# Postponing the first norm's sums and the first column's evacuation in a two-block kernel on one core

## The reference

```
def rmsnorm(u, g):
    r = rsqrt(mean(u * u, axis=-1) + 1e-6)
    return u * r * g

h = rmsnorm(x, g[0])
z = h @ w_in                      # 2048 x 6144
hy = dwconv3(z[..., :3072], hy_short_w, hy_short_b)
x0, x1, v = split(hy, 3)
h_fwd, h_bwd = hyena_filters(...) # two small sin layers, then a wide one
y_a = x0 * two_sided_fftconv(v * x1, h_fwd, h_bwd, hy_bias)
gb, gc, xv = split(z[..., 3072:], 3)
y_b = gb * dwconv3(gc * xv, sc_conv_w)
m = concatenate([y_a, y_b]) @ w_out
```

## Time and profile before

| what | value |
|---|---|
| median of 3 runs | 2413.16 us (2412.05 to 2413.39) |
| time of the profiled execution | 2412.67 us |
| its span in the profile | 2410.8 us |
| PE busy | 2370.4 us (98%) |
| DVE busy | 1327.5 us (55%) |
| ACT busy | 1096.3 us (45%) |
| POOL busy | 27.7 us (1%) |
| mean granted PE clock | 0.995 of full speed |

### The profile page before, as it was taken

The page is one execution under the profiler, slowest core; times in us unless marked ns, Lnnn a source line. Parts: engine busy times, 40 slices in busy tenths (PEclk is TensorE's granted clock), DMA queues, the critical chain, the costliest instruction groups (busy, mean ns, idle before and its releaser), DMA issues.

```text
span 2410.8 us, 25538 instructions
## 1 busy us (share of the span) xinstructions
PE 2370.4 (98%) x11089; PEld 1961.8 (81%) x11089; DVE 1327.5 (55%) x1315; ACT 1096.3 (45%) x1159; POOL 27.7 (1%) x49
## 2 busy tenths in 40 slices
PE   7999999999999999999999999999999999999998
PEld 6778787788888888888888888888888878888887
DVE  5675855544544544556764454444454576555654
ACT  5444444544454344355555444344334356444443
POOL 1000000000000000000000000000000000000000
PEclk9999999999999999999999999999999999999999
DMA  7444455555555555555445555555555545643344
GB/s 283 170 156 182 176 203 196 181 187 192 192 202 188 187 190 192 192 188 209 184 176 187 192 192 186 191 183 191 192 192 185 190 149 190 248 148 140 122 149 148
DMA packets 63103, 446.08 MB, mean 185 GB/s; under 512 B 7209, under 2 KB 7540, under 8 KB 11215
## 3 DMA queue, kind: packets, MB, share of 16 engines
q1 hardware_dynamic: 60080, 427.60, 49.6%
q0 software_dynamic: 2912, 16.85, 1.9%
HBM read 442.33 MB, written 2.10 MB: 184 GB/s over the span
## 4 chain that ended last, share of the span: by engine, by line
PE 93%; DVE 3%; DMA 2%; ACT 2%; issue 1%; POOL 0%; ACTq 0%; POOLq 0%; SPq 0%; DVEq 0%
PE P L329 90%; PE P L332 3%; DVE raw_r L596 1%; ACT hi L487 1%; DMA raw<-in_w_i 1%; DVE R_h L583 0%; DMA raw<-in_w_z 0%; DMA raw<-in_w_d 0%; DVE X L583 0%; DVE EV L639 0%; ACT R_h L483 0%; DVE R_m L580 0%; DMA raw<-in_w_ukv 0%; ACT EV L509 0%; DMA raw<-in_w_u 0%
## 5 line engine op out<-in xcount | busy, mean ns | idle before, releaser
L596 DVE TENSOR_TENSOR raw_r<-raw,hi 128x2048 fp32r<-128x2048 f32 (+3 forms) x412 | 928.4, 2256 | 954.4 <-ACT hi L487 953.8
L329 PE MATMUL P<-hi,R_h 128*128 128x512 f32 (+2 forms) x3840 | 1231.9, 395 | 17.9 <-DVE raw_r L596 10.9
L487 ACT ACTIVATE hi<-raw 128x2048 fp32r<-128x2048 f32 (+3 forms) x412 | 776.4, 1887 | 1010.9 <-DMA raw<-in_w_d 390.3
L329 PEld LDWEIGHTS P<-hi,R_h 128*128 128x128 f32 x3840 | 725.5, 189 | 169.9 <-DVE R_h L583 18.1
L329 PE MATMUL P<-hi,R_f_r 128*128 128x512 f32 x2480 | 777.0, 391 | 0.1
L329 PE MATMUL P<-raw_r,R_h 128*128 128x512 f32 (+2 forms) x1920 | 748.3, 390 | 0.0
L329 PEld LDWEIGHTS P<-hi,R_f_r 128*128 128x128 f32 x2480 | 465.7, 188 | 96.5 <-DVE raw_r L596 0.5
L329 PE MATMUL P<-raw_r,R_f_r 128*128 128x512 f32 x1240 | 482.7, 389 | 0.0
L329 PEld LDWEIGHTS P<-raw_r,R_h 128*128 128x128 f32 x1920 | 363.7, 189 | 73.0 <-issue 3.8
L329 PEld LDWEIGHTS P<-raw_r,R_f_r 128*128 128x128 f32 x1240 | 232.9, 188 | 47.3
L332 PE MATMUL P<-ident,EV 128*128 128x128 f32 (+2 forms) x486 | 72.6, 272 | 0.0
(11 more groups left out here) (187 smaller groups left out, 838.4 us busy)
## 6 DMA issues: line engine op xcount, KB each, us to landing
raw<-in_w_u SPq DMA_DIRECT2D x128, 1024.0 KB, 4.8
raw<-in_w_d SPq DMA_DIRECT2D x128, 1024.0 KB, 4.8
raw<-in_w_z SPq DMA_DIRECT2D x48, 1024.0 KB, 4.8
raw<-in_w_i SPq DMA_DIRECT2D x36, 1024.0 KB, 4.8
raw<-in_w_mo SPq DMA_DIRECT2D x16, 1024.0 KB, 4.8
raw<-in_w_o SPq DMA_DIRECT2D x16, 1024.0 KB, 4.7
raw<-in_w_mkv SPq DMA_DIRECT2D x8, 1024.0 KB, 4.7
R_g<-in_rows POOLq DMA_DIRECT2D x6, 1024.0 KB, 5.7
```

The source lines that it names most:

```text
L329: return self.e.matmul(o, l, r, start=start, stop=stop, skip_group_check=True)
L487: self.e.activation(hi, raw, ACT.Copy).then_inc(*self.inc("high_made", ("high", k, d)))
L596: self.e.tensor_tensor(low, raw, hi.bitcast(f32), ALU.subtract).then_inc(*self.inc("low_made", *names))
```

## The change

Two things move. `first_sums` gets two more nops ahead of it, and the first column no longer does a `flush` and an `evac` at its end: its evacuation becomes a piece of `later`, behind `first_sums`, and puts two nops and the two turns of column 0 at the head of the list when it is done. As column 1 follows at once, the pieces fall so: column 1: s1 to s3 nops, s4 `first_sums`, s5 evacuation of column 0, s6, s7 nops, s8 the first turn of column 0, and `flush` at the end does the second. `evac` of column 1 follows. Nothing of `extra` is reached in column 1. Column 2: s1, s2 turns of column 1, s3 `load_bias`, s4 `filter_1`, s5 to s7 nops, s8 `filter_2`; then `evac` of column 2. Column 3: s1, s2 turns of column 2, s3 to s5 nops, s6 to s8 the first three `filter_3`. So all of `extra` comes four steps later until it is used up.

```
-    later += [...first_squares...] + [first_reduce, nop, nop, nop, nop, first_sums]
+    later += [...first_squares...] + [first_reduce] + [nop] * 6 + [first_sums]
...
     for n, kind in enumerate(kinds):
         banks, done = gemm("w_z", HH, HL, h_m, 16, 512, steps=2)
+        if n == 0:
+            def first_out(banks=banks, done=done):
+                ks, ms = evac(banks, done, scale_m=list(r1_m))
+                later[0:0] = [nop, nop] + [lambda c=c: mixer_turn("gc", c, ks, ms) for c in (0, 2)]
+            later.append(first_out)
+            continue
         flush()
         if n == 7:
             flush_all()
         ks, ms = evac(banks, done, scale_m=list(r1_m))
-        later += [nop] * {0: 2, 8: 1, 9: 1, 10: 1}.get(n, 0)
+        later += [nop] * {8: 1, 9: 1, 10: 1}.get(n, 0)
```

More of the change, by code:

```diff
@@ L1300, in conduct @@
             split_ahead(g + 1)
-    later += [lambda g=g: first_squares(g) for g in range(4)] + [first_reduce, nop, nop, nop, nop, first_sums]
+    later += [lambda g=g: first_squares(g) for g in range(4)] + [first_reduce] + [nop] * 6 + [first_sums]
     side_load("c6", m.f_w3, a["w_f3"], xt_m[3])
```

## The result

The changed kernel takes 2416.77 us (median of 22 runs, 2410.86 to 2422.17), the kernel before in the same series 2413.36 us (22 runs, 2409.41 to 2418.70). The ratio is 1.0016, with a 95% interval of 1.0008 to 1.0023: 3.4 us more by the medians, less than the 0.2% (4.8 us) that I had set as the bound.

A forecast was written before the change was run, and what follows sets the result against it. PE, busy for 98% of the span, bounds the kernel; only its waits and low clock can be won. Gains of 8.37 us against costs of 9.99 gave +1.6, so 2414.8 us, range 2411.0 to 2418.3.

The forecast's parts named there:

- The win: Column 1 starts 5.95 us earlier and 13 matmuls escape the low clock, 2.42 us: together 8.37 us won.
- Step 1: first_sums, put back in the middle of column 1 among warm products, costs 0.45 us, between 0.42 and 0.85.
- Step 2: PE's block 5 still waits for DVE's low part behind the reduction: 1.57 us, 1.4 idle, no clock fall.
- 24% that I gave to a fall: Rival: the clock also falls after the first gap, near 39, costing 1.7 to 3.4 us more; middle 2417.1 us.
- Step 3: Norm's chain: rstd on DVE at 49.7, column 0 evacuated 51.3 to 52.6, first turn near 57.3; hidden by 4.7 us.
- rival of the late tile: Tile 8 lands late, so column 0's evacuation and column 1's turn stall PE: 6.2 us, 2421.0 us; chance 7%.
- Step 4: Two gc copies on ACT ahead of column 1's evacuation delay the turn in column 2: 0.3 us, bounds 0 and 0.8.
- Step 5: filter_2's sine on ACT holds up column 2's evacuation, so PE waits for its turn: 5.07 us, bounds 4.6 and 5.6.
- Step 6: Low clock behind the gap at column 2's turn: 2.6 us, between 1.7 and 3.4.
- Step 7: All later pieces of extra come four steps later, in the same order and distances: costs nothing.
- The sum: Costs of 9.99 us against 8.37 won: +1.6 us, 50% as written; its own range 2412.8 to 2417.0 us.
- uncertainty of 1.7 us either way: Falls of the clock after the later gaps can shift the time by some 1.7 us either way.

The follow-up runs named there:

- version 4: Changed kernel with three nops ahead of first_reduce, the sums one step later, and one more nop ahead of filter_2: 2405.84 us, ratio 0.9970.
- second profile: Profile from rerunning the changed kernel unchanged, as a control: 2416.94 us (6 runs), ratio 1.0026.
- experiment 7: Changed kernel with filter_2 one step earlier, at s7 of column 2, all behind it unmoved: 2409.69 us, ratio 0.9990.
- experiment 5: Changed kernel with 18 matmuls whose result nothing reads, on PE ahead of the first transpose of column 2: 2415.56 us, ratio 1.0015.
- experiment 11: Second series of the changed kernel with 18 unread matmuls ahead of the first transpose of column 2: 2413.14 us, ratio 1.0006.
- experiment 1: Changed kernel with one more nop ahead of filter_2, which then comes at s3 of column 3: 2407.48 us, ratio 0.9980.
- experiment 2: Kernel before with filter_2 alone moved from s4 to s8 of column 2 by four more nops: 2418.87 us, ratio 1.0037.
- experiment 6: Kernel before with 20 filling matmuls ahead of first_sums, in the gap of 4.95 us: 2411.91 us, ratio 1.0000.
- experiment 3: Changed kernel with three nops ahead of first_reduce, so it follows tile 6's low part, and the sums one step later: 2415.42 us, ratio 1.0013.
- its control: Kernel before, rerun unchanged: 2412.13 us, ratio 0.9997.
- experiment 12: Second series of the kernel before with 20 filling matmuls ahead of first_sums: 2411.24 us, ratio 0.9998.

## Why the prediction was right, point by point

**The win.** The gap of 4.95 us and the low stretch are gone from their place as forecast; version 4, which has no gap in either place, shows the whole: 7.85 us less in the first stretch, where 8.37 - 0.45 = 7.92 follow from the forecast's terms.

**Step 1, first_sums warm:** 0.36 us for 0.45, and below the 0.42 that I had as its least.

**Step 2, the first gap:** idle 1.20 us for 1.4, no fall of the clock, 1.4 in the second profile, none either. But its length is not a constant. It was 1.61, 1.91, 2.31 and 2.51 us in four experiments that hadn't touched this place (7, 5, 11 and 1). On DVE the reduction begins behind the low part of tile 4, and that tile lands at different times: the reduction began at 30.43 and 30.59 us in the two profiles of the changed kernel, and at 30.95, 31.65, 32.24 and 32.41 in these four. In three of the four the clock fell. The 24% that I gave to a fall was rather too little, and that it didn't fall in either profile of the changed kernel is in part luck.

**Step 3, the norm's chain, hidden:** DVE's first operation at 50.30 (49.7 forecast), evacuation of column 0 from 51.94 (51.3), the turn at 57.23. Tile 8 was asked for at 39.09 and its high part began at 46.14, so the rival of the late tile didn't come. Column 0's turn had 4.0 us left (its evacuation ended at 53.2).

**Step 4, the two copies ahead of column 1's evacuation:** PE's products let it have the turn at 60.61 + 0.23 = 60.84, the evacuation ended at 60.92, and the turn came at 61.06: 0.22 us for 0.3.

**Step 5, the second gap:** with E, the end of column 2's products, at 81.91, the high part came at E - 0.43 (-0.37 forecast), the low part at E + 1.51 (1.57), the evacuation at E + 6.97 (7.04), the transpose at E + 8.36 (8.43). The stall is 90.27 - 85.44 = 4.83 us for 5.07. Experiments 1, 2 and 7 show the cause: the gap goes with `filter_2`'s place, comes without the norm's change, and shrinks when one tile's split stands between the sine and the evacuation. The Trainium skill, in "TensorE: Matmul & The Clock Gate", section "Architectural detail: the array is 16× 32×32, not 1× 128×128", has ScalarE's queue as strictly in order; the trace agrees, with ACT idle for 5.17 us while a finished column lay in PSUM.

**Step 6, the clock behind it:** the turn took 91.01 - 90.27 = 0.74 us for 0.36, the next twelve products 5.09 for 2.87 at the full clock (82.57 to 85.44): 2.60 us for 2.6. Experiments 5 and 11, with filling products in the gap, have 3.22 us from transpose to transpose instead of 5.83, and took 2.2 +- 0.8 us back in the time.

**Step 7, all else of the extra list:** costs nothing that can be seen; experiment 1 keeps all of it four or five steps late and has no other gap. Nor has the changed kernel a third one up to 410 us.

**The sum:** the first stretch is 1.3 us longer (1.1 to 1.8 over all pairs of profiles), +1.6 were forecast. The bounds of the steps add up to 8.3 at the low end and not to 8.0, so that range begins at 2413.1 us. The time is 3.4 us longer, and with 2416.77 us the median is 2.0 above the 2414.8 of the forecast. That it still lies inside the summed range, which ends at 2417.0, owes something to luck: what moved it isn't among the steps. It is what the clock does later in the run. I had it as an uncertainty of 1.7 us either way; in both profiles of the changed kernel some 3 us are lost beyond the first stretch against the profile of the kernel before (the span is 4.4 and 4.3 us longer), and both have falls of the clock near 417, 1222, 1946 and twice between 2236 and 2253 us. The kernel before has them near 433, 1222, 1946 and 2235 in one profile and near 433, 2235 and 2245 in the other. Over all fourteen profiles of this document the part beyond the first stretch takes 2115.3 to 2120.8 us and goes along with the time at the lower level there while PE has products, 6.8 to 20.4 us (correlation 0.89).

The averages go the same way: over 28 runs the changed kernel is 5.4 us longer at the lower level than the kernel before over 89, which at 0.35 us of time for each (the slope over the runs of either kernel) is 2 us. With so many runs that is more than chance. Why a kernel whose later part is the same instruction by instruction should fall more often there is not settled. The postponed evacuation by itself isn't it: experiments 1 and 4 have it too, and their profiles have the shortest later parts of all (2115.3 and 2116.8 us, against 2117.4 and 2117.9 for the kernel before), while experiment 6 doesn't have it and took 2120.2. The three profiles that have both the postponed evacuation and an idle second gap (the changed kernel twice, and experiment 3) all took 2120.7 to 2120.8; whether the one follows from the other, no run shows. For one version, a series of six to eleven runs can't tell a habit from chance.

## What to carry to other kernels

Side work has two lengths: how long it takes, and how long it holds up what is queued behind it on each engine. A small matmul whose result goes over DVE to ACT kept ACT from its next piece for 7 us; it cost nothing in the middle of a column and 4.83 + 2.60 = 7.4 us at its end, just ahead of the evacuation that PE wanted 12 products later. So when work is postponed, everything that is listed behind it moves too, and the place where each piece lands has to be looked at: here one nop was worth 7 us where it acts, and 8.6 in the time. And a gap should be closed altogether, since what is left of it is longer in some runs (1.20 to 2.51 us here) and can still bring the lower clock.

## What the runs showed of the hardware

The reduction of 128x4096 took 7.25 to 7.29 us in the three profiles in which PE idled through much of it (the kernel before, its control and experiment 2), and 7.49 to 7.60 in all those where PE went on with products for most or all of it. The kernel before is among the first, and experiments 6 and 12, which add nothing to it but PE's filling products, among the second (7.55 and 7.49). Why PE's work should slow this instruction isn't shown.

The clock fell to the lower of its two levels after idle gaps of PE of 1.54, 1.91, 2.31 and 2.51 us in the experiments (at 39.9, 41.7, 42.8 and 42.5), and stayed up after gaps of 1.12, 1.20, 1.37 and 1.61. So the length of a gap alone doesn't decide: 1.54 and 1.61 went different ways, and so did one and the same gap of 1.90 us (below). The Trainium skill, in "TensorE: Matmul & The Clock Gate", section "HAM oscillation — how this bites in real kernels", speaks of waits of about 3 to 5 us; here less was enough. The gap of 1.90 us at 1220 us is in each profile of the two kernels; in one of the four, the control of the kernel before, the clock stayed up behind it. The same holds for the gap of 2.02 to 2.04 us near 1943.

Two falls of the changed kernel show that a long gap isn't needed either. At 416.7 the clock fell behind a gap of 0.96 us, which had eight transposes and a gap of 0.42 ahead of it; the kernel before has nearly the same rows there (0.51 and 0.95) and kept the clock. And at 2236.0 it fell while PE had no wait at all, 2.3 us into a group of 32 small matmuls. PE's timeline:

```profile
2233.67 4.67 PE L329 MATMUL P<-cols,R_s 96*128 96x15 f32 x32
```
